# First norm of a two-block transformer kernel: the root is taken out of the input and put where products leave PSUM

## The chip, the cores and the metric

The kernel runs on one core of one Trainium2 chip. The metric is the device time of one execution in microseconds. Three executions of the kernel before gave 791.43 to 791.72 us, median 791.57 us.

## The reference, cut to what matters

Two transformer blocks follow each other, on 256 tokens of width 1024. Only the entry of the first block is touched:

```python
def rmsnorm(x, g):
    xf = x.astype(jnp.float32)
    y = xf * lax.rsqrt(jnp.mean(xf * xf, axis=-1, keepdims=True) + EPS)
    return (y * g.astype(jnp.float32)).astype(x.dtype)

u = rmsnorm(h, norm_mix_g[layer])
p = jnp.einsum('bsd,de->bse', u, w_in[layer]) + b_in[layer]
aq, ak, av, hq, hf, hi, hg, gate_a, gate_b = split_columns(p)
```

The attention branch takes aq, ak, av; the recurrent branch takes silu(hq), sigmoid(hf), hi and sigmoid(hg); sigmoid of the two gates weighs the branches. The root of a token is one factor for all columns of its row of p, so it may be applied to x or to the product.

## The kernel before

**Operands.** All products are float32 made of three fast ones: each operand is split into a rounded high part and the low rest (wH and wL of the weights, p1H and p1L of the normed input, turned so that channels lie on partitions), and wH x p1H, wH x p1L and wL x p1H are added in PSUM. ScalarE rounds the high part (split_hi, line 762, or first_hi, 776, for the first panels), VectorE subtracts it for the low part (split_lo, through the helper at line 1173).

**Panels.** A weight matrix is read in groups of 512 columns (kv has 256), each in two panels of four 128-row blocks. `timeline()` writes the order of all events out, and each engine runs through that list: at a panel, ScalarE and VectorE split the weights of the panel that comes two later (AHEAD = 2), TensorE multiplies, and at `evac` a group's tiles leave PSUM. So on VectorE the evacuation of a group stands behind the split that was listed at the group's last panel. The first groups are q0, q1, kv, ga0, ga1, hq0, hf0, hi0, hg0, gb0, gb1, hq1, hf1, hi1, hg1, then the branch products ba0, ba1 and so on; between them stand the steps of the attention (scores, scale, pt, pv) and of the recurrence (hprep, hA to hD).

**Evacuation of the first product.** Groups with channels on partitions (q, kv, hq, hf) are taken out of PSUM by ScalarE alone, with bias and function in one instruction: Identity for q (911), Identity for k and v and the shifted copy aKS of k (918), Sigmoid and Identity for hq (933, 935), two Sigmoids for hf (943, 945). Groups with tokens on partitions (hi, hg, ga, gb) are taken out by VectorE with a row of biases added (1376), and a Sigmoid on ScalarE follows for three of them.

**The entry.** SyncE loads x as two halves of 128 tokens, waits for the first, and then issues the first weights (596 to 605). ScalarE squares x and takes the roots (793, 836), TensorE turns x against the identity and spreads the roots over all partitions (1760, 1764), VectorE multiplies turned input, gain and root into TMP (1280), ScalarE rounds it to p1H (888), VectorE subtracts for p1L (1261). The order of these steps and of the first eight weight blocks is written out in the three `norm(0)`.

**Waits that matter below.** The scores of the first attention unit wait on TensorE for q1, for aKS and for aK (lines 1994 to 1996), right behind the last panel of kv. The transposes `pt` of a unit wait for its normed probabilities from VectorE. hA waits for the last product of hprep (2061). A weight slot of wH is one of three, and is free when the panel three before is done. VectorE's event `setup` prepares a small weight block dtW for the second block of the model.

Of the kernel before, what the change touches and what calls it, by code (L numbers as in the profile page):

```python
# [6 lines left out]
F32 = mybir.dt.float32  # L7
# [4 lines left out]
ALU = mybir.AluOpType  # L12
AX_X = mybir.AxisListType.X

P = 128
# [44 lines left out]
for _i in range(2):  # L60
    for _name, _c in (("q", 0), ("hq", 1280), ("hf", 2304)):
        GROUPS[f"{_name}{_i}"] = group("w_in", [(_c + _i * W, W)],
                                    cm_tiles(4 * _i if _name in ("q", "hf") else 0, 2 * _i if _name == "hq" else 0), "AAAA", "P1")
# [8 lines left out]
GROUPS["kv"] = group("w_in", [(1024, 256)], [("cm", 0, 0), ("cm", 1, P)], "AA", "P1")  # L72
# [7 lines left out]
for _name, _c in (("z", 0), ("xs", 512), ("bc", 1024), ("q2", 1544), ("k2", 2056)):  # L80
# [20 lines left out]
          "ga1": (1, 5376 + W), "hi1": (1, 3328 + W), "hg1": (1, 4352 + W)}  # L101
ROWS = 32
# [27 lines left out]
def timeline():  # L130
# [33 lines left out]
    gemm("q0")  # L164
# [47 lines left out]
def build(nc, IN, out):  # L212
# [17 lines left out]
    with ExitStack() as ctx:  # L230
# [60 lines left out]
        on.in_x = [ctx.enter_context(nc.semaphore(f"in_x{j}")) for j in range(TB)]  # L291
# [87 lines left out]
        TILE, USED, EV, SILU, SIGMOID = {}, {}, {}, {}, {}  # L379
        tiles = plain = 0  # L380
        ev = {"A": 0, "D": 0}
        for name, part in panels:
            g = GROUPS[name]
            if part == len(g["parts"]) - 1:
                for m in range(len(g["tiles"])):
# [6 lines left out]
                    if name[:2] in ("ga", "gb", "hg"):  # L392
                        ev["A"] += 1
                        SIGMOID[name, m] = (on.evac_act, ev["A"])
# [46 lines left out]
        vT, dtw, ext = scr(11, T), scr(10.5, KD, 8), scr(40, 384)[0:8]  # L441
# [53 lines left out]
        rbs = scr(69, T)  # L495

# [15 lines left out]
        HALVES = {"out1": (on.merged, 8), "down1": (on.tmp_done, 16), "oo1": (on.pt_done, 9), "dd1": EV["u9", 2]}  # L512
# [31 lines left out]
        def un(k):  # L544
            return ps[:, 4, wide(1)] if k == 7 else ps[:, 4 + k // 2, wide(k % 2)]

# [47 lines left out]
        def _(sp):  # L594
            for j in range(TB):
                sp.dma_start(res[:, j], IN["x"][0, j * P:(j + 1) * P, :]).then_inc(on.in_x[j], 16)
            sp.wait_ge(on.in_x[0], 16)
            first = IN["w_in"][0].rearrange("(k p) n -> p k n", p=P)
            for k in range(KP):
# [6 lines left out]
            for i, (kind, q) in enumerate(stream):  # L606
# [26 lines left out]
                if i == 3:  # L633
# [3 lines left out]
                    sp.dma_start(dtw, IN["w_in_2"][0].rearrange("(k p) n -> p k n", p=P)[:, :, 1536:1544]).then_inc(on.in_dtw, 16)  # L637
# [6 lines left out]
                if kind == "w" and panels[q] == ("f1", 0):  # L644
# [4 lines left out]
                    sp.wait_ge(on.hs_done, 4)  # L649
                    sp.dma_start(gfin, IN["norm_final_g"][0:1, :].partition_broadcast(P)).then_inc(on.in_gain, 16)  # L650
# [16 lines left out]
        def _(pool):  # L667
# [49 lines left out]
            for e in TL:  # L717
# [8 lines left out]
                elif e[0] == "hprep" and e[2] == 3:  # L726
                    if e[1]:
                        pool.wait_ge(on.o_psum, 2 * e[1])
                    else:
                        pool.wait_ge(on.aks, 2)  # L730
                        pool.wait_ge(on.dtw_lo, 1)
# [5 lines left out]
        def _(act):  # L737
# [50 lines left out]
            def square_x(j):  # L788

                act.wait_ge(on.in_x[j], 16)  # L790
# [59 lines left out]

            def norm(n):

                table(ACT.Sqrt)
                for j in range(TB):
# [4 lines left out]
                    elif n:  # L859
                        square(n, 1, j)  # L860
                    else:
                        square_x(j)
# [5 lines left out]
                if n == 0:  # L868
                    first_hi(0, 0, 1)
# [3 lines left out]
                for k in range(KD):  # L873
                    if n == 2 and k == 0:
                        ada_copy(1)
                    if n == 0 and 0 < k < 4:
                        first_hi(0, k, 1)
                    elif n == 0 and k in (4, 5):
                        first_hi(1, 2 * k - 8, 2)
                    elif n == 3 and 1 < k <= KP + 1:  # L880
# [5 lines left out]
                    act.wait_ge(on.tmp_done, 8 * n + k + 1)  # L886
# [15 lines left out]
            def evac(name):  # L902
# [10 lines left out]
                if g == "q" and name in ("q0", "q1"):  # L913
                    each(lambda m: aQ[:, 4 * i + m], ACT.Identity, bias=lambda m: pc("b_in", 4 * i + m))
                elif name == "kv":
                    act.wait_ge(on.tile_done, TILE[name, 0])
                    for b in range(2):
                        nc.scalar.activation(aKS[C * b:C * b + C], ps[C - C * b:P - C * b, 0, 0:T], ACT.Identity,
# [1316 lines left out]
```

## Time and profile before

| | before |
|---|---|
| time, median of 3 runs | 791.57 us |
| time of the profiled execution | 791.62 us |
| span of the profiled execution | 789.9 us |
| outside the span | 1.7 us |
| TensorE busy, share of the span | 98% |
| VectorE busy | 77% |
| ScalarE busy | 61% |
| mean granted TensorE clock | 0.999 |

The span runs from the first to the last instruction of the profile, 1.7 us lie around it. A share of busy time is a mean over stages with different limits. Matmuls overlap in the pipeline: one with 256 columns lasts 0.28 us by the profile, but starts follow each other by 0.12 us.

### The profile page before, as it was taken

How to read it: one execution, taken by the hardware profiler on the slowest of the kernel's cores; microseconds unless marked ns; L12 is line 12 of the kernel's file. 1: busy time of each engine (PE TensorE's matmuls, PEld its weight loads, DVE VectorE, ACT ScalarE, POOL GpSimd, SP SyncE). 2: the span in 40 equal slices, each digit the busy share in tenths (PEclk: the TensorE clock that was granted, in tenths of full speed). 3: DMA queues.
4: the chain of work that ended last, by engine and by line, in shares of the span. 5: the costliest groups of instructions: out<-in, count | busy, mean ns of one | idle time of the engine just before them, and what ended most of it. 6: DMA issues, size and time to landing. Idle time of an engine off the chain costs nothing. (4 is left out here: it accounts for less than half of the span.)

```text
span 789.9 us, 12522 instructions
## 1 busy us (share of the span) xinstructions
PE 776.6 (98%) x5048; PEld 686.5 (87%) x5048; DVE 606.3 (77%) x815; ACT 483.5 (61%) x733; POOL 18.0 (2%) x38
## 2 busy tenths in 40 slices
PE   8999999999999999999999999999999999999996
PEld 7978978898888898888888888999789999999885
DVE  5587787887887667887869897997878787777464
ACT  6877888468644374444334367876858667665451
POOL 3000001000200000000000000001000000000000
PEclk9999999999999999999999999999999999999999
DMA  8873634656546638799879994644363756555711
GB/s 303 295 262 126 226 124 158 189 206 219 173 161 211 213 110 273 273 306 315 274 240 339 335 372 132 230 129 139 107 213 109 239 175 200 167 171 171 240 53 54
DMA packets 106537, 162.54 MB, mean 206 GB/s; under 512 B 4576, under 2 KB 51824, under 8 KB 106480
## 3 DMA queue, kind: packets, MB, share of 16 engines
q1 hardware_dynamic: 106336, 161.48, 60.6%
q8 instruction: 40, 0.66, 0.3%
q10 hardware_dynamic: 144, 0.26, 0.1%
q14 instruction: 17, 0.14, 0.0%
HBM read 160.67 MB, written 1.06 MB: 205 GB/s over the span
## 5 line engine op out<-in xcount | busy, mean ns | idle before, releaser
L1173 DVE TENSOR_TENSOR wL<-raw,wH 128x2048 fp32r<-128x2048 f32 (+2 forms) x142 | 284.6, 2009 | 86.5 <-ACT wH L762 83.6
L762 ACT ACTIVATE wH<-raw 128x2048 fp32r<-128x2048 f32 (+1 forms) x114 | 212.0, 1863 | 86.5 <-PE ps L1864 57.7
L1861 PE MATMUL ps<-p1H,wH 128*128 128x256 f32 x784 | 223.9, 286 | 2.0 <-DVE arena L1173 0.8
L1861 PE MATMUL ps<-p1H,wL 128*128 128x256 f32 x784 | 221.2, 283 | 0.0
L1861 PE MATMUL ps<-p1L,wH 128*128 128x256 f32 x784 | 219.8, 283 | 0.0
L1861 PEld LDWEIGHTS ps<-p1H,wH 128*128 128x128 f32 x784 | 150.2, 192 | 5.7 <-issue 2.1
L1861 PEld LDWEIGHTS ps<-p1H,wL 128*128 128x128 f32 x784 | 150.2, 192 | 0.0
L1861 PEld LDWEIGHTS ps<-p1L,wH 128*128 128x128 f32 x784 | 149.5, 192 | 0.0
L1864 PE MATMUL ps<-wH,p1H 128*128 128x512 f32 x316 | 125.2, 396 | 0.0
L1864 PE MATMUL ps<-wL,p1H 128*128 128x512 f32 x316 | 123.2, 390 | 0.0
L1864 PE MATMUL ps<-wH,p1L 128*128 128x512 f32 x316 | 123.1, 390 | 0.0
L1864 PEld LDWEIGHTS ps<-wH,p1H 128*128 128x128 f32 x316 | 59.4, 188 | 12.8 <-issue 0.7
L1864 PEld LDWEIGHTS ps<-wL,p1H 128*128 128x128 f32 x316 | 59.3, 188 | 12.7
L1864 PEld LDWEIGHTS ps<-wH,p1L 128*128 128x128 f32 x316 | 59.4, 188 | 11.6
L1864 PE MATMUL ps<-wH,zH 128*128 128x512 f32 x168 | 65.4, 389 | 0.0
L1864 PE MATMUL ps<-wH,zL 128*128 128x512 f32 x168 | 65.4, 389 | 0.0
L1864 PE MATMUL ps<-wL,zH 128*128 128x512 f32 x168 | 65.4, 389 | 0.0
L1176 DVE SCALAR_TENSOR_TENSOR arena<-arena,par 128x256 f32<-128x256 f32 x116 | 47.5, 482 | 8.2 <-ACT arena L985 7.3
L1176 DVE SCALAR_TENSOR_TENSOR arena<-raw,cact,arena 128x512 f32<-128x512 f32 x56 | 42.0, 751 | 1.7
L1864 PEld LDWEIGHTS ps<-wL,zH 128*128 128x128 f32 x168 | 31.5, 188 | 6.6
L1864 PEld LDWEIGHTS ps<-wH,zH 128*128 128x128 f32 x168 | 31.5, 188 | 6.6
L1864 PEld LDWEIGHTS ps<-wH,zL 128*128 128x128 f32 x168 | 31.5, 188 | 6.4
(304 smaller groups left out, 953.3 us busy)
## 6 DMA issues: line engine op xcount, KB each, us to landing
raw<-in_w_in SPq DMA_DIRECT2D x37, 1024.0 KB, 5.8
raw<-in_w_ada SPq DMA_DIRECT2D x24, 1024.0 KB, 5.3
raw<-in_w_up SPq DMA_DIRECT2D x44, 512.0 KB, 4.7
raw<-in_w_ffn_gate SPq DMA_DIRECT2D x22, 512.0 KB, 4.4
raw<-in_w_ffn_up SPq DMA_DIRECT2D x22, 512.0 KB, 5.5
raw<-in_w_ffn_down SPq DMA_DIRECT2D x10, 1024.0 KB, 6.2
raw<-in_w_down SPq DMA_DIRECT2D x10, 1024.0 KB, 5.0
raw<-in_w_out SPq DMA_DIRECT2D x8, 1024.0 KB, 5.0
```

Of the source, the lines that this page charges most:

```text
L762: nc.scalar.activation(wH[:, q % NHL, 0:nk, 0:wd], raw[:, i % NRAW, 0:nk, 0:wd], ACT.Copy).then_inc(on.w_hi, 1)
L1173: return v.tensor_tensor(o, a, b, op)
L1176: return v.scalar_tensor_tensor(out=o, in0=a, scalar=s, in1=b, op0=op0, op1=op1)
L1861: last = mm(ps[:, t[1], 0:T], wt[:, slot, k, t[2]:t[2] + P], at_[:, k0 + k, :], start=st, stop=en)
L1864: last = mm(ps[:, t[1], 0:t[3]], at_[:, k0 + k, t[4] * P:(t[4] + 1) * P], wt[:, slot, k, t[2]:t[2] + t[3]], start=st, stop=en)
```

## The change

The input is turned and rounded with its gain but without its root; the root row is spread later and multiplied in where the products of the first matrix are evacuated.

- SyncE: x comes in four quarters of 256 channels (1 KB per token), each issued ahead of one of the first four weight blocks; the wait for x is gone. The small load dtw moves from the first loads to a place among the panels of f.
- Entry (`enter`): per 128 channels ScalarE reads the turned x from PSUM with the gain as scale into p1H, VectorE makes p1L by one scalar_tensor_tensor; the products with TMP and the root are gone. TensorE turns quarter c behind block c - 1 of q0.
- Roots (`root`): behind the first panel of q0 in the list; Sqrt table load, two squares, two roots on ScalarE. TensorE spreads them behind tile 1 of q1's first panel and then waits until ScalarE has copied the row (rb_copy) at the head of `evac q0`.
- Evacuation: q, kv, hq and hf are first multiplied by the root row on VectorE (PSUM to SBUF); ScalarE then works on SBUF. hq's bias and product become four scalar_tensor_tensor. hi, hg, ga, gb become scalar_tensor_tensor with the token's root as scalar. The scores wait for ScalarE's second step of q1 and kv, and aKS is copied last.

```diff
-GROUPS["kv"] = group("w_in", [(1024, 256)], [("cm", 0, 0), ("cm", 1, P)], "AA", "P1")
+GROUPS["kv"] = group("w_in", [(1024, 256)], [("cm", 0, 0), ("cm", 1, P)], "DD", "P1")
-    gemm("q0")
+    gemm("q0", [("root",)])
# SyncE
-            for j in range(TB):
-                sp.dma_start(res[:, j], IN["x"][0, j * P:(j + 1) * P, :]).then_inc(on.in_x[j], 16)
-            sp.wait_ge(on.in_x[0], 16)
             for k in range(KP):
+                sp.dma_start(res[:, :, wide(k)], x[:, :, wide(k)]).then_inc(on.in_x[k], 16)
                 sp.dma_start(raw[:, 0, k, :], first[:, k, 0:W]).then_inc(on.in_w0[k], 16)
# ScalarE
+            def enter():
+                act.wait_ge(on.in_par, 16)
+                for k in range(KD):
+                    if k % 2 == 0:
+                        act.wait_ge(on.ut_psum, k // 2 + 1)
+                    if k == 1:
+                        first_hi(0, 1, 1)
+                    nc.scalar.activation(p1H[:, k], xT(k), ACT.Copy, scale=gain(0, k)).then_inc(on.uh_done, 1)
+                    if k in (0, 1, 2):
+                        first_hi(0, (0, 2, 3)[k], 1)
+                    elif k in (3, 5):
+                        first_hi(1, k - 3, 2)
+            def root_0():
+                table(ACT.Sqrt)
+                for j in range(TB):
+                    square_x(j)
+                    root(0, j)
...
-                    each(lambda m: aQ[:, 4 * i + m], ACT.Identity, bias=lambda m: pc("b_in", 4 * i + m))
+                    if i == 0:
+                        act.wait_ge(on.rb_psum, 1)
+                        nc.scalar.activation(rbs0, rb, ACT.Copy).then_inc(on.rb_copy, 1)
+                    for m in range(4):
+                        act.wait_ge(*EV[name, m])
+                        nc.scalar.activation(aQ[:, 4 * i + m], aQ[:, 4 * i + m], ACT.Identity,
+                                             bias=pc("b_in", 4 * i + m)).then_inc(on.evac_act, 1)
                 elif name == "kv":
+                    for m, t in enumerate((aK, vT)):
+                        act.wait_ge(*EV[name, m])
+                        nc.scalar.activation(t, t, ACT.Identity, bias=pc("b_in", 8 + m)).then_inc(on.evac_act, 1)
+                    act.wait_ge(*SECOND[name, 0])
                     for b in range(2):
+                        nc.scalar.activation(aKS[C * b:C * b + C], aK[C - C * b:P - C * b], ACT.Copy).then_inc(on.aks, 1)
...
                     for m in range(4):
+                        act.wait_ge(*EV[name, m])
+                        nc.scalar.activation(T2[:, m], T1[:, m], ACT.Sigmoid, scale=-1.0,
+                                             bias=negb[:, 4 * i + m:4 * i + m + 1])
+                        nc.scalar.activation(T1[:, m], T1[:, m], ACT.Sigmoid,
+                                             bias=pc("b_in", 18 + 4 * i + m)).then_inc(on.evac_act, 1)
# VectorE
+                for k in range(KD):
+                    if k < 4:
+                        first_lo(0, k, 1, k == 3)
+                    elif k in (4, 6):
+                        first_lo(1, k - 4, 2, k == 6)
+                    dve.wait_ge(on.uh_done, k + 1)
+                    stt(p1L[:, k], xT(k), gain(0, k), p1H[:, k].bitcast(F32), ALU.mult, ALU.subtract).then_inc(on.u_ready, 1)
...
+                if name in ROOTED and GROUPS[name]["tiles"][0][0] == "cm":
+                    if name == "q0":
+                        dve.wait_ge(on.rb_copy, 1)
+                    for m, t in enumerate(GROUPS[name]["tiles"]):
+                        dve.wait_ge(on.tile_done, TILE[name, m])
+                        tt(to[m], ps[:, t[1], 0:T], rbs0, ALU.mult).then_inc(on.evac_dve, 1)
                 if g == "hq":
+                    for m in range(4):
+                        dve.wait_ge(*SECOND[name, m])
+                        ins = stt(hQ[:, m], hQ[:, m], pc("b_in", 10 + 4 * i + m), SQ[i][:, m], ALU.add, ALU.mult)
...
-                        tt(to, ps[:, GROUPS[name]["tiles"][j][1], :], rows(name)[0], ALU.add).then_inc(on.evac_dve, 1)
+                        stt(to, ps[:, GROUPS[name]["tiles"][j][1], :], R1[:, j:j + 1], rows(name)[0], ALU.mult,
+                            ALU.add).then_inc(on.evac_dve, 1)
# TensorE
+                        if q == 0 and k < 3:
+                            turn_input(k + 1)
+                        if (name, part, m) == ("q1", 0, 1):
+                            spread_roots(0)
+                            pe.wait_ge(on.rb_copy, 1)
...
-                        pe.wait_ge(*EV["q1", 3])
+                        pe.wait_ge(*SECOND["q1", 3])
                         pe.wait_ge(on.aks, 2)
-                        pe.wait_ge(*EV["kv", 0])
+                        pe.wait_ge(*SECOND["kv", 0])
```

## Rows read from the trace of the kernel before

**Rows 1.** Part 1 of the page: busy us, share of span, instructions.
```profile
PE 776.6 (98%) x5048; PEld 686.5 (87%) x5048; DVE 606.3 (77%) x815; ACT 483.5 (61%) x733; POOL 18.0 (2%) x38
```
**Rows 2.** Waits of TensorE: waiting line, releaser, us in total, times, longest.
```profile
PE ps L1802 <- ACT arena L911: 0.8, 1, 0.8
PE ps L1861 <- DVE p1L L1173: 0.7, 1, 0.7
```
**Rows 3.** Timeline of the opening: start us, duration, engine, line, operation.
```profile
4.31 1.06 ACT L793 ACTIVATE arena<-res 128x1024 f32<-128x1024 f32 x1 [2.00 <-DMA res<-in_x]
...
6.86 0.29 ACT L836 ACTIVATE R<-XS,eps 128x1 f32<-128x1 f32 x1
...
9.26 0.36 PE L1861 MATMUL ps<-p1H,wH 128*128 128x256 f32 x1
...
22.39 0.38 PE L1861 MATMUL ps<-p1H,wH 128*128 128x256 f32 x1
```
**Rows 4.** DMA issues of the opening: count, KB of one, median us to landing.
```profile
raw<-in_w_in SPq DMA_DIRECT2D x1, 256.0 KB, 2.7
...
raw<-in_w_in SPq DMA_DIRECT2D x2, 512.0 KB, 6.4
```
**Rows 5.** Timeline of ScalarE from 20 to 31 us, and TensorE's first scores.
```profile
20.79 1.90 ACT L762 ACTIVATE wH<-raw 128x2048 fp32r<-128x2048 f32 x1
22.59 1.55 ACT L911 ACTIVATE arena<-ps,par 128x256 f32<-128x256 f32 x4
...
25.86 1.28 ACT L1024 ACT_TABLE_LOAD   x1
...
30.41 1.04 ACT L762 ACTIVATE wH<-raw 128x1024 fp32r<-128x1024 f32 x1
...
40.68 0.59 PE L1802 MATMUL ps<-mask,identb 128*128 128x512 bf16 x2 [0.77 <-ACT arena L911]
```
**Rows 6.** VectorE's instructions of the first 60 us by form: busy us, mean ns.
```profile
L1173 DVE TENSOR_TENSOR wL<-raw,wH 128x1024 fp32r<-128x1024 f32 x9 | 10.9, 1224 | 5.8 <-ACT wH L762 5.2 <-ACT wH L758 0.5
L1173 DVE TENSOR_TENSOR wL<-raw,wH 128x2048 fp32r<-128x2048 f32 x4 | 9.2, 2292 | 3.0 <-ACT wH L762 3.0
L1173 DVE TENSOR_TENSOR p1L<-arena,p1H 128x256 fp32r<-128x256 f32 x8 | 3.4, 427 | 0.2 <-ACT p1H L888 0.2
...
L1176 DVE SCALAR_TENSOR_TENSOR acc<-raw,cact,acc 128x512 f32<-128x512 f32 x4 | 3.0, 751 | 0.1
L1173 DVE TENSOR_TENSOR wL<-raw,wH 128x512 fp32r<-128x512 f32 x4 | 2.8, 688 | 0.5 <-ACT wH L776 0.5
```
**Rows 7.** Timeline of VectorE around the evacuation of hf0.
```profile
97.47 2.29 DVE L1173 TENSOR_TENSOR wL<-raw,wH 128x2048 fp32r<-128x2048 f32 x1 [3.07 <-ACT wH L762]
...
107.27 0.69 DVE L1173 TENSOR_TENSOR arena<-arena,RD 128x512 f32<-128x512 f32 x1
```
**Rows 8.** Timeline of ScalarE and TensorE in the same stretch.
```profile
101.27 0.52 ACT L945 ACTIVATE arena<-ps,negb 128x256 f32<-128x256 f32 x1
...
108.36 1.03 PE L1760 MATMUL ps<-ident,arena 128*128 128x128 f32 x8
```
**Rows 9.** Timeline of VectorE, ScalarE and TensorE from hf1 to hA(1).
```profile
181.07 2.29 DVE L1173 TENSOR_TENSOR wL<-raw,wH 128x2048 fp32r<-128x2048 f32 x1
...
196.07 2.29 DVE L1173 TENSOR_TENSOR wL<-raw,wH 128x2048 fp32r<-128x2048 f32 x1 [2.93 <-ACT wH L762]
...
209.49 1.21 DVE L1173 TENSOR_TENSOR arena<-arena 128x1024 f32<-128x1024 f32 x1
...
185.29 1.92 ACT L762 ACTIVATE wH<-raw 128x2048 fp32r<-128x2048 f32 x1
...
211.68 1.15 PE L2071 MATMUL ps<-arena 128*64 128x64 f32 x32
```
**Rows 10.** Stretches at the end: busy us by engine, granted clock, DMA share, GB/s.
```profile
783.00:784.00 1.00, 0.60 (x6) 0.39 (x4) 0.93 (x4) 0.43 (x3) 0.00 (x0) 1.00 0.00 0
...
788.00:789.00 1.00, 0.00 (x0) 0.00 (x0) 0.00 (x0) 0.00 (x0) 0.00 (x0) 0.58 0.99 377
```

More of the change, by code:

```diff
@@ L101 @@
           "ga1": (1, 5376 + W), "hi1": (1, 3328 + W), "hg1": (1, 4352 + W)}
+ROOTED = ["kv"] + [f"{_n}{_i}" for _i in range(2) for _n in ("q", "hq", "hf", "hi", "hg", "ga", "gb")]
 ROWS = 32
@@ L290, in build @@
         on.in_rel = ctx.enter_context(nc.semaphore("in_rel"))
-        on.in_x = [ctx.enter_context(nc.semaphore(f"in_x{j}")) for j in range(TB)]
+        on.in_x = [ctx.enter_context(nc.semaphore(f"in_x{c}")) for c in range(4)]
         on.lb_diff = ctx.enter_context(nc.semaphore("lb_diff"))
@@ L495, in build @@
         rbs = scr(69, T)
+        rbs0 = dtW[:].rearrange("p k n -> p (k n)")
         adarow = TMP[:, 0:2].rearrange("p a n -> p (a n)"), scr(60, W)
@@ L788, in square_x @@
             def square_x(j):
-                act.wait_ge(on.in_x[j], 16)
+                for c in range(4):
+                    act.wait_ge(on.in_x[c], 16)
                 if j:
@@ L1472, in tail @@
                     tt(zL[:, 2 * i:2 * i + 2], zps if i in TOKENS_FIRST else ZT, zH[:, 2 * i:2 * i + 2].bitcast(F32), ALU.subtract).then_inc(on.z_ready, 1)
+                    if i == 5:
+                        dve.wait_ge(on.in_dtw, 16)
+                        step(v.memset(dtW[:], 0.0))
+                        v.tensor_copy(dtW[:, :, 0:8], dtw).then_inc(on.dtw_lo, 1)
                 elif g == "u":
@@ L1787, in late_turn, with turn_input, spread_roots @@
             def late_turn(n, k):
-                pe.wait_ge(*((on.rb_copy, n + 1) if k == 6 else (on.tmp_done, 8 * n + 2)))
+                pe.wait_ge(*((on.rb_copy, n + 1) if k == 6 else (on.tmp_done, 8 * (n - 1) + 2)))
                 turn(n, (k,), range(TB)).then_inc(on.ut_psum, 1)
+            def turn_input(c):
+                pe.wait_ge(on.in_x[c], 16)
+                if c > 1:
+                    pe.wait_ge(on.u_ready, 2 * c - 2)
+                for k in (2 * c, 2 * c + 1):
+                    for j in range(TB):
+                        last = tr(xT(k)[:, j * P:(j + 1) * P], res[:, j, k * P:(k + 1) * P])
+                last.then_inc(on.ut_psum, 1)
+            def spread_roots(n):
+                for j in range(TB):
+                    pe.wait_ge(on.rd_done, 2 * n + j + 1)
+                    last = spread(rb[:, j * P:(j + 1) * P], R1[:, j:j + 1])
+                last.then_inc(on.rb_psum, 1)
             def gate_sum(g, i):
@@ L1892, in panel @@
                         early = k == 0 and name in NORM_OF
-                        if early:
+                        if q == 0 and k == 0:
+                            pe.wait_ge(on.uh_done, 1)
+                            pe.wait_ge(on.first_hi, 1)
+                            for t in g["tiles"]:
+                                product(t, 0, only=(0,))
+                        elif early:
                             pe.wait_ge(on.uh_done, 8 * NORM_OF[name] + 1)
@@ L1905, in panel @@
                                 pe.wait_ge(on.gate_done, 2 if name == "f0" else 4)
-                            last = product(t, k, only=(0, 2) if early else (0, 1, 2))
+                            last = product(t, k, only=(2,) if early and q == 0 else (0, 2) if early else (0, 1, 2))
                         if early:
```

136 lines of the change are left out of this document (53 added, 83 removed).

## The prediction

> **What bounds the kernel now.** I read the busy shares first: TensorE 98%, VectorE 77%, ScalarE 61% [rows 1]. So TensorE is the bound, and what an edit is worth is read from TensorE's gaps. The opening timeline came next: the first product starts at 9.26 us, and q1 starts at 22.39 us [rows 3]. q0 has 96 products at a spacing of 0.12 us, 11.5 us of work, between 9.26 and 22.2 us: 1.4 us of gaps, of which TensorE's waits show 0.7 for the low part of the input [rows 2]. Then the matmul starts of the first 260 us, one after another: they follow each other without a gap, but for 0.8 us at the first scores [rows 2, 5] and 0.6 us at one pt. A gain can therefore only come from the first 22 us, and everything after it is covered by very little: each wait that is put between a last product and the next step of TensorE costs its full length. The last thing read was where VectorE and ScalarE stand in the list when a group's last tile is done, since the change puts both of them, in turn, between PSUM and the consumer.
>
> **The entry: what is gained.** x landed at 4.31 us as a half of 512 KB, and the first roots were done at 6.86 + 0.29 us [rows 3]. A load of 256 KB into an idle queue landed after 2.7 us [rows 4], so the first quarter, issued at 0.8 us, lands at 3.5; quarters and weight blocks alternate behind it at 0.3 to 0.35 MB/us, which puts the last block of q0's first panel at 9.5 to 10.2 us and the two halves of its second panel at about 11.5 and 13 us (before, these two were issued at 6.57 and 7.05 and took 6.4 us, 12.5 and 13.9 [rows 4]). ScalarE then rounds eight channel blocks (0.42 us each, by the like of p1L, 0.43 [rows 6]) and six weight pieces (0.6 or 1.05 us) and is through at 15.0 us. VectorE has four splits of 0.69 us, two of 1.22 and eight of 0.43 to 0.48 [rows 6] and follows at 16.5. TensorE works one block behind, pays 1.5 us for three groups of four turns inside q0, and ends q0 at 20.0 us instead of 22.2. **Gain 2.2 us**, between 1.2 (1 KB packets that are slower) and 3.0. A table load that now stands ahead of the first Copy could cost up to 1.28 us [rows 5], of which the loads hide most; I take nothing. TensorE's wait for rb_copy inside q1 is new: two spreads, ScalarE's copy of 0.37, and two signals of 0.15 to 0.25, together 1.1 us (0.8 if ScalarE is ready, 2 if it is late). That leaves 1.1 us gained, if nothing else stood in the way.
>
> **The chain through q0, q1 and kv: what is lost.** Before, ScalarE's work from 20.79 us on was: split for q1 (1.90), four evacuations of q0 as soon as the tiles were there (22.59, 1.55), a wait for data, a split, three table loads of 1.28 with small instructions from 25.86 to 30.41, the split for kv's second panel, the evacuations of q1, two large splits [rows 5]. It was ready just in time: TensorE waited 0.8 us and began the scores at 40.68 [rows 2, 5]. After, in the same order:
> - ScalarE: end of the entry 15.0, the two halves for q1 to 17.0, Sqrt load 1.28, squares and roots 2.84 (4.31 to 7.15 before [rows 3]) to 21.15, split for q1's second panel to 23.05.
> - VectorE splits the low part of that panel (2.29 [rows 6]) to 25.4 and only then evacuates q0, four of 0.36 to 0.43; ScalarE adds the biases behind it, to 27.5 (24.1 before).
> - Split for kv 28.5; the vectors, 4.55 us with their three loads, 33.1 (30.4 before); split 34.1. VectorE's split for kv's second panel ends at 35.3 and the evacuation of q1 at 36.8, ScalarE's biases at 37.2.
> - Two large splits, 39.05 and 40.95; VectorE's two behind them end at 41.3 and 43.5. These stand in the list before kv's evacuation.
> - VectorE takes aK out, 43.9, and v, 44.3; ScalarE biases both, 44.8, copies aKS in two halves of 0.48, 45.8; the signal to TensorE takes 0.2.
> TensorE has ended kv at 38.5 and idles until 46.0, where before it went on at 40.68. **Net loss 5.3 us**, gain and rb wait of the entry included; TensorE is not in this chain, so a faster or slower entry moves it only with ScalarE's 15.0: 4.3 to 6.5. What hides the extra evacuations before was that ScalarE had 2.2 us of waits for data and TensorE there; they are used up.
>
> **The clock.** TensorE's clock was granted in full (2.4 GHz) everywhere, also over the gaps of 0.8 us. At the end it fell to its lower level, 1.2 GHz, in the stretch from 788 us, while the last product lies in the stretch from 783 [rows 10]: some 4.7 us of idling went before it. A gap of 7.5 us is longer, so the scores and part of ga0 would run at the lower level. No row shows it rise again. Bounds: nothing, or half speed over the scores and ga0's first panel (1.7 and 5.7 us of work, up to 3.7 with the signals between). **I take 1.5 us**, the nearer end being the short one since products follow densely. The Trainium skill (TensorE: Matmul & The Clock Gate, What's actually happening) says that the throttled state is the default and activity releases it; the fall in the rows agrees, and by that rule the term cannot be nothing.
>
> **Evacuations with a scalar.** ga, gb, hi, hg: scalar_tensor_tensor of 512 columns took 0.75 us where a two-operand form took 0.69 [rows 6]: 0.1 us per group pair on the way to the probabilities of a unit; it shows only where pt already waited, after ga0: **0.2 us**. The Trainium skill (Vector Engine (DVE) Microarchitecture Reference, Points that are easy to get wrong) says scalar_tensor_tensor with two float32 sources in SBUF halves the rate; the 0.75 against 0.69, both with two such sources, does not show that. By the rule hq's four would add 1.5 us more per group.
>
> **hq0 and hf0.** hq0 costs nothing: VectorE is free to evacuate it right behind its split, ScalarE has one Sigmoid per tile instead of two instructions, and the product ends where it did. hf0 differs. VectorE's split ends at 99.76 [rows 7]; only then come four multiplies, and ScalarE's eight Sigmoids (0.36 apart) run from 100.3 to 103.2 instead of ending at 101.79 [rows 8]. Queued behind them on ScalarE are the attention output, the Exp load, half a split and the exponentials: the probabilities of unit 4, ready at 107.96 [rows 7], come at 109.2, and TensorE's second four transposes want them at 108.75 [rows 8]. **0.7 us**. The lag, less that stall, reaches unit 5: **0.4 us** (0 to 0.8).
>
> **hq1 and hf1.** hq1 is evacuated behind a split on VectorE; ScalarE's next split moves from 173.8 to 175.7, an ada step of VectorE follows, and the split at 181.07 [rows 9] moves by 1.9. hf1's multiplies start at 185.3, where ScalarE's old evacuation was already over, and ScalarE's eight Sigmoids end at 188.7: its split at 185.29 [rows 9] starts 3.4 us late. The whole chain behind it (Ln, scans, Exp, splits) is serial: the split at 196.07 moves to 199.5, ready at 201.8, for hg1's second panel that TensorE starts at 200.95 (two panels of 5.47 us ahead of hA at 211.68 [rows 9]): 1.0. ba0 0.6, and the product at 209.49 comes 3.8 late, for hA: 1.3. **2.9 us** (0.5 to 4).
>
> **Moved and hidden.** dtw's load and the making of dtW (0.5 us of VectorE) go to the stage of f, where every group waits on TensorE: nothing, up to 0.5 if a weight load behind the small packets is late. POOL loses a wait: nothing.
>
> **Sum,** against the profiled execution: span 789.9 + 5.3 + 1.5 + 0.2 + 0.7 + 0.4 + 2.9 = 800.9, with 1.7 around it 802.6; the median lies 0.05 below the profiled execution: **802.5 us**.
>
> **Rivals.**
> - The hand-offs are hidden and the entry's gain stands: 791.6 - 2.2 + 1.1 = 790.5, not slower. It decides at one point: aKS and aK must be ready when kv's last product ends, 7.3 us earlier than my chain has them. For it: ScalarE is busy only 61% [rows 1]. Against: in this stretch it has no such reserve, 0.8 us of wait stood there already. 0.09; an entry near 3.0 makes it faster by over 0.2%, which is 0.05 of it.
> - Only the first hand-off costs: VectorE's and ScalarE's slack behind it (2.93 us of waiting before 196.07 [rows 9]) takes up hf0 and hf1, and the clock costs 0.7: 791.6 + 5.3 + 0.7 = 797.6. 0.15.
> - The opening does not speed up, because quarters with 1 KB rows crowd the first weights: ScalarE's entry ends 1.5 us later and the chain with it: 804.0. 0.08.
> - The clock stays low over a whole panel more and hg1's weights cascade into the following panels: 807. 0.08.
> - My forecast: 0.60.
>
> **How the numbers follow.** The range reaches from 796.0 (second rival, with the entry's chain 1 us shorter) to 806.5 (forecast with the clock at its upper bound and the chain at its own). A change of 0.2%, 1.6 us, is about what a measurement of this kernel tells from none. Slower by over that: 0.91; within: 0.04; faster: 0.05.
>
> **What would show it.** Right: q1's first product at about 20.2 us; a pause near 23 us with ScalarE's copy behind it; TensorE idle for 6 to 8 us before the scores, released by ScalarE's copy of aKS, and VectorE's kv evacuation directly behind a split of 2.29 us; a stretch below full clock behind it; new waits at pt(4), at hg1 and at hA. Wrong: no gap over 3 us before the scores would fell the largest term, and with it the sign.

## The result, and the profile after

The changed kernel took **805.56 us** (median of 4 executions, 803.31 to 806.20) against 791.50 us before: a ratio of 1.017, 95% interval 1.0158 to 1.0183, slower by 14 us. The forecast was 802.5 with a range of 796.0 to 806.5. The profiled execution, which all traces below are read from, took 803.31 us, with a span of 801.6 against 789.9: 11.7 us longer.

The page's part 1 after the change, to be held against [rows 1] (TensorE had 776.6 us):

```profile
PE 780.3 (97%) x5044; PEld 688.8 (86%) x5044; DVE 611.7 (76%) x839; ACT 482.1 (60%) x725; POOL 22.2 (3%) x38
```

TensorE is busy 3.7 us longer with about as many instructions, and the rest is idling. Its waits, as in [rows 2] (waiting line, releaser, us in total, times, longest):

```profile
PE ps L1857 <- ACT arena L947: 6.4, 1, 6.4
...
PE ps L1916 <- ACT wH L779: 1.7, 1, 1.7
PE ps L1919 <- DVE wL L1193: 1.4, 1, 1.4
...
PE ps L1916 <- ACT dtW L936: 0.5, 1, 0.5
```

One wait of 6.4 us, for ScalarE's copy of aKS (L947), stands where 0.8 stood. The timelines of VectorE, ScalarE and TensorE around it (start, duration, engine, line, operation), which answer to [rows 5]:

```profile
40.76 4.49 DVE L1193 TENSOR_TENSOR wL<-raw,wH 128x2048 fp32r<-128x2048 f32 x2 [1.56 <-ACT wH L765]
45.17 0.75 DVE L1193 TENSOR_TENSOR arena<-ps,dtW 128x256 f32<-128x256 f32 x2
...
45.62 0.91 ACT L944 ACTIVATE arena<-arena,par 128x256 f32<-128x256 f32 x2 [3.09 <-DVE arena L1193]
46.56 0.85 ACT L947 ACTIVATE arena<-arena 64x256 f32<-64x256 f32 x2
...
47.66 1.01 PE L1857 MATMUL ps<-mask,identb 128*128 128x512 bf16 x2 [6.36 <-ACT arena L947]
```

TensorE's last product of kv starts at 41.03. Its tiles lie in PSUM while VectorE makes two splits of 2.29 us for the next weights, then VectorE takes them out, then ScalarE adds the biases, then ScalarE copies aKS. And the opening, against [rows 3]:

```profile
4.89 1.06 PE L1800 MATMUL ps<-ident,res 128*128 128x128 f32 x4
...
8.49 1.20 PE L1916 MATMUL ps<-p1H,wH 128*128 128x256 f32 x4 [1.69 <-ACT wH L779]
9.48 1.05 PE L1916 MATMUL ps<-p1H,wL 128*128 128x256 f32 x4
...
6.06 1.28 ACT L863 ACT_TABLE_LOAD   x1 [6.06 <-PE ps L1800]
7.36 0.47 ACT L863 ACTIVATE p1H<-ps,par 128x256 fp32r<-128x256 f32 x1
```

The first product starts 0.8 us earlier than before (8.49 against 9.26), but q1 starts at 22.70, 0.3 later. Four products take 1.0 us here and the next four 0.86, 0.21 to 0.25 each, where the same form is spaced by 0.12 from 11.9 us on.

### The profile page after: what moved, and what is told of

Same layout as the page of the kernel before. It is cut to its first block and busy times, and to the rows that moved or that the text cites. A ratio compares the mean times of both kernels' runs of the same rounds, so it can differ in the third digit from the quotient of the medians.

```text
span 801.6 us, 12537 instructions
## 1 busy us (share of the span) xinstructions
PE 780.3 (97%) x5044; PEld 688.8 (86%) x5044; DVE 611.7 (76%) x839; ACT 482.1 (60%) x725; POOL 22.2 (3%) x38
## 5 line engine op out<-in xcount | busy, mean ns | idle before, releaser
L1919 PEld LDWEIGHTS ps<-wH,p1L 128*128 128x128 f32 x316 | 59.6, 189 | 11.7
L1196 DVE SCALAR_TENSOR_TENSOR arena<-arena,par 128x256 f32<-128x256 f32 x124 | 50.8, 480 | 8.2 <-ACT arena L1003 7.3
```

Source lines behind the costliest of these rows:

```text
L1196: return v.scalar_tensor_tensor(out=o, in0=a, scalar=s, in1=b, op0=op0, op1=op1)
L1919: last = mm(ps[:, t[1], 0:t[3]], at_[:, k0 + k, t[4] * P:(t[4] + 1) * P], wt[:, slot, k, t[2]:t[2] + t[3]], start=st, stop=en)
```

## Experiments

Diffs are against the kernel named. The kernel before was run on the same chip each time (medians 791.59 to 791.74).

**e1_fill.** Is the slow stretch behind the gap the clock, and what is it worth? The changed kernel with 26 idle products (identity by identity) in the gap:

```diff
                     elif u:
                         pe.wait_ge(on.probs, 2 * u)
+                    if u == 0:
+                        warm(26)
                     if kind == 1:
                         pe.wait_ge(on.consts, 1)
```

> The changed kernel with 26 idle products (identity against identity) on TensorE between the last product of kv and the waits of the first scores; nothing else is touched. Theory (the clock is a term of its own): the granted clock stays at its upper level through the gap, the scores and ga0's first panel take their old times (1.8 and 5.6 us instead of 3.3 and 6.3), so the profiled span falls by about 2.2 us, to 799.4; and since the mean granted clock of the four executions of the changed kernel ran from 0.990 to 0.995 with times of 806.2 to 803.3, the spread goes too: all executions near 801. The gap itself stays, the scores start at 47.7 us. Rival (the low clock costs nothing, the spread has another cause): median 805.5, spread as before.

Measured: 803.0 us (802.77 to 803.6), ratio 1.0143 (1.0128 to 1.0158), 2.5 less than the changed kernel. The granted clock by stretch (us of the span, length, busy us of five engines, clock, DMA share, GB/s), first the changed kernel, then this one:

```profile
40.00:46.00 6.00, 1.31 (x11) 1.10 (x10) 5.16 (x4) 2.91 (x3) 0.00 (x0) 0.97 0.49 171
46.00:53.00 7.00, 5.34 (x26) 3.92 (x27) 2.13 (x5) 3.11 (x9) 0.00 (x0) 0.54 0.59 226
```
```profile
40.00:46.00 6.00, 6.00 (x55) 5.86 (x53) 5.16 (x4) 2.88 (x4) 0.00 (x0) 1.00 0.50 160
46.00:53.00 7.00, 6.14 (x40) 4.82 (x40) 3.88 (x8) 4.47 (x20) 0.00 (x0) 1.00 0.53 199
```

With the gap idle, the clock is granted at 0.54 in the stretch behind it; with the gap filled it stays at 1.00, and scores and ga0's first panel take 1.81 and 5.6 us again (3.29 and 6.29 in the changed kernel). The price of the clock in the profiled execution is shown, 2.2 us. The spread between executions, four of each, falls from 2.9 to 0.8 us, which fits that the clock made a good part of it. The scores start at 46.91 and not at the 47.7 that I expected, since q1 starts 1.1 us earlier in this execution than in that of the changed kernel, with the same opening (see e10_opening). The profiled span is only 0.6 shorter, though: the 2.4 us that stood at pt(5) were mostly used up by waits for hg1's weights (1.7 instead of 1.4), for hA (0.9, see the last section) and for a root at 487 us (0.7). My 801 was 2 us too low.

**e2_out_first.** The chain through kv: VectorE takes kv, hq and hf tiles out ahead of the split that stands before them in the list (`rooted` holds the multiplies that stood in `evac`).

```diff
+            FIRST_OUT = ("kv", "hq0", "hf0", "hq1", "hf1")
...
+                    if e[1] in FIRST_OUT and e[2] == 1:
+                        rooted(e[1])
                     if q < len(panels) and e[1:] not in LATER and e[1:] not in BESIDE:
                         split_lo(q)
```

> The changed kernel, but VectorE multiplies the tiles of kv, hq and hf out of PSUM ahead of the weight split that the list has at the group's last panel, not behind it. Theory (VectorE's queue order costs): kv's tiles come out 2.2 us earlier, so TensorE's gap ahead of the scores is 4.2 instead of 6.4 us; the stall at pt(4), 0.8 us, and the one at hg1's second panel, 1.5 us, go; with the shorter low clock median 800 to 802. Rival (ScalarE's chain through q0 and q1 alone sets all of it): at most 0.7 us less than 805.5.

Measured: 800.22 us (798.4 to 801.21), ratio 1.0104 (1.0087 to 1.0121); span 796.7.

```profile
PE ps L1866 <- ACT arena L947: 4.2, 1, 4.2
...
PE ps L1809 <- DVE arena L1193: 1.2, 4, 0.4
```

The gap is 4.2 instead of 6.4, as expected, and the wait for hg1's weights is gone. So 5.3 us of the median (4.9 of the span) came from the place of five evacuations behind a split, and not from the extra work itself. Two things limit this. Up to 0.75 us of the span is the faster opening of this execution (q1 at 21.63 against 22.70; with the same start e1_fill has its scores 0.75 earlier). And the waits at the pt steps, which I expected to lose pt(4)'s, are 1.2 us in all, four of them, where the changed kernel has 0.6. The clock falls behind this gap too: the scores take 3.10 us (44.39 to 47.49).

**e3_vectors_late.** The other piece of that chain: the small vectors with their three table loads (and the setup behind them) moved from q1 to behind ga0's first panel.

```diff
-    gemm("q1", [("vectors",)], [("setup",)])
+    gemm("q1")
-    gemm("ga0", Y(0), X(1, "ga1", 0))
+    gemm("ga0", [("vectors",), ("setup",)] + Y(0), X(1, "ga1", 0))
```

> The changed kernel with the events vectors and setup (three table loads, 4.55 us of ScalarE) moved from q1 to behind ga0's first panel. Theory (ScalarE's serial work through q0, q1 and kv sets the scores): ScalarE reaches the large splits 2.6 us earlier and is then bound by q1's and kv's products, the scores start at 45.0 instead of 47.7 us, TensorE's gap is 3.8 us, short enough for the clock to stay up: median 798.5 to 801. Rival (VectorE's splits ahead of kv's evacuation set it, ScalarE has slack): 805.

Measured: 808.41 us, ratio 1.0207 (1.0192 to 1.0222), worse than the changed kernel.

```profile
PE ps L1800 <- DVE arena L1193: 4.8, 3, 3.9
PE ps L1857 <- ACT arena L947: 4.0, 1, 4.0
```

The gap shrank to 4.0 as expected (scores at 45.77), but pt(1) now waits 3.9: the loads end at 61.1 on ScalarE, and the attention output, the Sigmoids of ga0 and the Exp load are queued behind them. The chain was read rightly and the new place badly; the expectation failed. It failed on the clock as well: I had called a gap of 3.8 us short enough, but behind the 4.0 us here the scores take 3.29 us (45.77 to 49.06), as behind the 6.4 of the changed kernel, and the clock from 46 to 51 us is granted at 0.50. Behind the 1.4 us of e7_combined they take 1.81.

**e4_entry** and **e10_opening.** Where did the entry's 2.2 us go? e4_entry puts a Sqrt table load ahead of everything and takes 3 idle products instead of 6 ahead of the first turned quarter; e10_opening also puts 8 instead of 2 behind it.

```diff
             act.wait_ge(on.pool_step, 3)
+            table(ACT.Sqrt)
...
-                        warm(6)
+                        warm(3)
                         turn_input(0)
-                        warm(2)
+                        warm(8)        # e10_opening alone; 2 in e4_entry
```

> The changed kernel with the Sqrt table loaded ahead of every wait of ScalarE, and three instead of six idle products ahead of the first turn of the input. Theory (the entry was late by the table load of 1.28 us that stood behind its waits, by the idle products that kept TensorE 1.2 us beyond the landing of x, and pays a second load at the roots): the first p1H starts at 5.7 instead of 7.4 us, ScalarE's chain is 2.9 us shorter, the scores start at 44.8, median 801 to 803. Rival (the first weights' landing bounds the entry): 805.

> The changed kernel with nothing but its opening altered: Sqrt table first, 3 idle products ahead of the first turned quarter and 8 (not 2) behind it, so that TensorE is not idle for the 1.2 to 1.7 us ahead of its first real product. Against e4_entry only the 8 differ. Theory: the opening's gain was real and was lost to the low clock; q1 starts at 21.0 (e4_entry 21.9, the changed kernel 22.7, the kernel before 22.39) and the first 12 products are 0.12 us apart. The hand-offs behind it are those of the changed kernel, so the time is 802 to 804: q1's earlier start shows in the scores by at most 1 us. Rival 'the first products wait for the rounding of their panels whatever the clock': q1 at 21.7 or later.

Measured: e4_entry 803.78 us (802.7 to 804.59), ratio 1.0147 (1.013 to 1.0164); e10_opening 802.63 (801.86 to 803.37), ratio 1.0138 (1.0124 to 1.0152). TensorE's opening, e4_entry first:

```profile
6.76 1.19 PE L1917 MATMUL ps<-p1H,wH 128*128 128x256 f32 x4 [1.24 <-ACT wH L779]
7.75 1.05 PE L1917 MATMUL ps<-p1H,wL 128*128 128x256 f32 x4
8.60 1.05 PE L1917 MATMUL ps<-p1L,wH 128*128 128x256 f32 x4
```
```profile
4.51 3.11 PE L1810 MATMUL ps<-ident 128*128 128x128 f32 x16
7.38 0.72 PE L1917 MATMUL ps<-p1H,wH 128*128 128x256 f32 x4
7.94 0.64 PE L1917 MATMUL ps<-p1H,wL 128*128 128x256 f32 x4
8.42 0.64 PE L1917 MATMUL ps<-p1L,wH 128*128 128x256 f32 x4
...
20.44 0.28 PE L1917 MATMUL ps<-p1H,wH 128*128 128x256 f32 x1
```

In e4_entry the first product starts 0.6 us sooner than in e10_opening and its twelfth product ends 0.6 later, since its products are 0.21 to 0.25 apart and not 0.12. Idle products without a gap up to the first real one bring q1 to 20.44 (21.8 in e4_entry, 22.70 in the changed kernel, 22.39 before). So of the forecast's 2.2 us 1.95 exist.

The opening differs from execution to execution, though, and each of these figures is from one. With the unaltered opening of the changed kernel q1 starts at 21.63 in e1_fill and e2_out_first, at 21.70 in e6_entry_alone, at 22.70 in the changed kernel and at 23.18 in e3_vectors_late; in the first three only about eight products are slower than 0.12. The kernel before varies less: 22.39, and 21.98 and 22.16 with the same opening in e8_before_masks and e12_before2. With 8 idle products it starts at 20.44, 20.59, 20.83 and 20.97 (e10_opening, e9_combined2, e11_combined3, e7_combined), so the two groups stay apart. Of the 2.3 us between 22.70 and 20.44, some 1.1 us is the first product's earlier start (7.38 for 8.49), and the rest is pace that three of the five executions did not lose.

e10_opening's time falls by 2.9 us against the changed kernel, within what I expected, but the scores start 2.5 us earlier (45.18 for 47.66) where I had allowed 1. e4_entry missed: scores at 46.56, expected at 44.8. Both have one reason, in ScalarE and VectorE behind q0, e4_entry first:

```profile
25.34 0.38 ACT L936 ACTIVATE dtW<-ps 128x256 f32<-128x256 f32 x1 [3.15 <-PE ps L1805]
25.76 1.42 DVE L1194 TENSOR_TENSOR arena<-ps,dtW 128x256 f32<-128x256 f32 x4 [1.25 <-ACT dtW L936]
```
```profile
23.96 0.38 ACT L936 ACTIVATE dtW<-ps 128x256 f32<-128x256 f32 x1 [2.25 <-PE ps L1805]
24.38 1.42 DVE L1194 TENSOR_TENSOR arena<-ps,dtW 128x256 f32<-128x256 f32 x4 [0.35 <-ACT dtW L936]
```

ScalarE was early, and waited for TensorE to spread the root, which stands inside q1's first panel; VectorE waited for that copy. From there on the chain to the scores hangs on TensorE: from e4_entry to e10_opening both q1 and the scores come 1.38 us earlier. In the changed kernel VectorE did not wait there (its split ended behind the copy). With the rest out of the way ScalarE's entry is bound by the weight blocks: in e10_opening it waits 2.1 us for them in four places, in the changed kernel for none.

The low pace in the opening is the clock's, by this: in e3_vectors_late, whose opening is the changed kernel's, the granted clock of the stretches 9 to 11.5 and 11.5 to 13 us is recorded below 1.

```profile
9.00:11.50 2.50, 2.50 (x16) 2.30 (x15) 2.13 (x5) 0.87 (x2) 1.21 (x4) 0.71 1.06 403
11.50:13.00 1.50, 1.50 (x9) 1.50 (x9) 0.95 (x2) 1.49 (x4) 0.00 (x0) 0.50 1.04 386
```

**e5_handoff_alone** and **e6_entry_alone.** The change in two halves. e5: the kernel before, its own entry and root, with the changed kernel's hand-offs; VectorE multiplies by a tile of ones that stands for the spread root:

```diff
+                    step(v.memset(dtW[:], 1.0))
                     turn_over(n, 0)
...
+                    for m, t in enumerate(GROUPS[name]["tiles"]):
+                        dve.wait_ge(on.tile_done, TILE[name, m])
+                        tt(to[m], ps[:, t[1], 0:T], rbs0, ALU.mult).then_inc(on.evac_dve, 1)
```

e6: the changed kernel's entry, late root and spread, with the evacuations of before; nothing multiplies by the root.

> The kernel before, with its own entry and its own root before the first product; only the evacuations are the changed kernel's (VectorE multiplies out of the banks by a tile that holds 1.0 everywhere, ScalarE follows in place, aKS is copied from the tile instead of from the bank, the gates keep the tensor_tensor of before). The output is the reference's. Theory: the second engine behind the attention tiles is the whole loss. Scores start at 45.5 to 46.5 instead of 40.68, TensorE's gap ahead of them is over 5 us and the granted clock falls once behind it; with 2.2 for the clock, 0.85 at pt(4) and 1.5 to 2 around hf1 and hA the time is 800 to 802. Rival 'the entry and the late root make part of it': 795 to 798, scores below 44. Rival 'the hand-off is hidden': 791.6 to 792.5.

> The other half alone: input in channel quarters, turned and rounded without its root, the root computed and spread inside q1 and copied by ScalarE behind q0; but the evacuations are those of the kernel before and nothing multiplies by the root (the output lacks it). Theory: the entry gains nothing (q1 starts at 22.4 to 22.9 against 22.39) since its first products run at the low clock, and the spread and its wait, 1.07 us on TensorE in q1, are mostly covered by the 1 us gap ahead of the scores: 791.6 to 793, scores at 41.0 to 41.8. Rival 'the entry is worth its 2.2 us where no hand-off follows': scores at 39.6 to 40, 790.0 to 790.5. Rival 'the entry is a loss by itself': 795 or more.

Measured: e5 802.04 us (801.45 to 802.26), ratio 1.0125 (1.011 to 1.014), span 799.9; e6 793.23 (791.99 to 794.43), ratio 1.0018 (1.0008 to 1.0027), span 790.3. TensorE's longest wait in e5:

```profile
PE ps L1811 <- ACT arena L925: 5.8, 1, 5.8
```

Scores start at 45.55 in e5 and 41.07 in e6. The hand-offs alone cost 10.0 us of span, the entry alone 0.4, both 11.7. Of the remaining 1.3, 0.75 is the opening of the profiled executions: q1 starts at 21.70 in e6 and at 22.70 in the changed kernel, and e1_fill, with it at 21.63, has the scores of the changed kernel 0.75 earlier. The other 0.5 may be that in e6 the later root and squares fall into ScalarE's slack, which in the changed kernel the hand-offs have used; this was not tested apart. By medians the halves cost 10.3 and 1.5 us and both 14.0. So the entry alone is a small loss clear of the noise, more than the 0.4 of its profiled execution, which was among the fastest of ten, and just outside the 793 that I had as its upper end.

**e7_combined, e9_combined2, e11_combined3.** Can the idea be made to pay? Everything found so far together: e2's order, e10's opening, the vectors' Sigmoids moved to ga0's own and their Silu and Exp behind kv, the spread one tile earlier, aKS copied ahead of v's bias. e9: only kv, hq1 and hf1 out first; the wait for the root's copy ahead of q1's fourth tile; the scores' masks ahead of the wait for aKS; the setup behind the first scores. e11 is e9 with ext, one piece of that setup, ahead of the scores again.

```diff
-    gemm("q1", [("vectors",)], [("setup",)])
+    gemm("q1")
-    gemm("kv", [], first[:-1] + [("v_turn",)] + first[-1:])
+    gemm("kv", [], [("vectors",), ("setup",)] + first[:-1] + [("v_turn",)] + first[-1:])   # e7, e11
+    gemm("kv", [], [("vectors",)] + first[:-1] + [("v_turn",)] + first[-1:])               # e9
-    gemm("ga0", Y(0), X(1, "ga1", 0))
+    gemm("ga0", Y(0), [("sign",)] + X(1, "ga1", 0))                                        # e7, e11
+    gemm("ga0", Y(0), [("setup",), ("sign",)] + X(1, "ga1", 0))                            # e9
```

> The changed kernel with everything that the runs pointed to: VectorE takes kv, hq and hf tiles out ahead of the split of the next weights; ScalarE's Sqrt table ahead of the entry and 3 idle products instead of 6, 8 instead of 2 behind the first turned quarter (to keep the clock up until the first product); the spread of the root one tile earlier in q1; the vectors' two Sigmoids moved to ga0's Sigmoids, their Silu and Exp and the setup behind kv's evacuation, where ScalarE idled 3.6 us; aKS copied ahead of vT. Theory: q1 starts at 20.5 to 21.5 (full clock from about 7 instead of 11.5), kv's products end at 40 to 40.5 and the scores start within 1 us of it; no low stretch of the clock behind kv; what is left is 0.9 at pt(4), 1 around hA, 0.2 for the gates: 790.5 to 793, that is level with the kernel before. Rival 'low clock of the opening is bound by idle time before 2.2 us, not by the gap': q1 at 21.9, 792 to 794. Rival 'the moved vectors collide with the Exp of the first scores': ga0 or its pt waits 1 to 2 us, 794 to 796.

> e7_combined with four repairs: only kv, hq1 and hf1 are taken out ahead of the split (in e7_combined TensorE waited 0.5 and 0.6 us in pt(3) and pt(4) for VectorE, which took hq0 and hf0 out first); the setup stands behind the first scores instead of ahead of them (it made VectorE 0.4 us late for their maximum); the wait for the root's copy stands ahead of q1's fourth tile instead of right behind the spread (0.47 us); the scores' masks are added ahead of the wait for aKS (0.6 us of the 1.4 us gap). Theory: 0.9 + 0.4 + 0.5 + 0.6 = 2.4 less than e7_combined's 794.7: 792.3, range 791.5 to 793.2, level with or 0.2% behind the kernel before. Rival 'the waits only move': 794 to 795.

> e9_combined2 with one thing put back: the part of the setup that makes ext stands ahead of the first scores again, since in e9_combined2 SyncE's queue of loads waited for it (ext_done) and stood still from 46 to 55 us (DMA share 0.01, TensorE waited 3.8 us in pt(1)); the rest of the setup stays behind the first scores. Theory: the 3.8 us and what they set off go: e9_combined2 stood 0.2 ahead of the kernel before at 54 us, and picks up 0.7 at pt(4) and 0.3 to 1 after it: 791.8 to 793, still not below the kernel before. Rival 'the late rest of the setup delays pt(0) as it did in e7_combined': 794 or more.

Measured: e7 794.69 us (794.06 to 794.88), ratio 1.0033 (1.0021 to 1.0045); e9 798.46, ratio 1.0085 (1.0071 to 1.0098); e11 793.21 (792.31 to 796.16), ratio 1.0024 (1.0014 to 1.0034). e9 missed by 6 us. A stretch of it, and the wait of the queue that issues the loads:

```profile
46.00:51.00 5.00, 4.02 (x21) 2.95 (x21) 4.64 (x9) 4.06 (x11) 0.00 (x0) 1.00 0.02 3
51.00:56.00 5.00, 5.00 (x36) 3.64 (x36) 4.89 (x6) 2.72 (x5) 0.00 (x0) 1.00 0.01 2
...
SPq L646 <- DVE arena L1578: 18.7, 1, 18.7
...
62.52 1.06 ACT L773 ACTIVATE wH<-raw 128x1024 fp32r<-128x1024 f32 x1 [3.49 <-DMA raw<-in_w_in]
```

SyncE stores ext and waits for it (L646) ahead of the next weights; with ext made behind the first scores, next to nothing was loaded for 10 us (DMA share 0.02 and 0.01) and ScalarE stood 3.5 us at 62 us. e11, which puts back that one piece, shows it: 5.3 us less. (e3_vectors_late had the same stall, 20.6 us at that wait and a DMA share of 0.01 from 46 to 61 us; there ScalarE was late by itself and hid it from me.) e11 still stands 1.5 us behind the kernel before: it starts the scores' products at 39.90, 1.3 us ahead of the 41.20 before, and loses the lead at the pt steps, where TensorE waits 2.2 us in all for VectorE, 0.3 and 0.7 of them in pt(0); before, 0.6. e7 came out above its expected 790.5 to 793: TensorE waits 1.4 us ahead of the scores and 2.0 at the pt steps.

**e8_before_masks** and **e12_before2.** Do the finds help the kernel before? e8 moves the masks of the first scores ahead of the wait for aKS, e12 also the vectors and the setup, much as in e7.

```diff
                         pe.wait_ge(*EV["q1", 3])
+                        if u == 0:
+                            masks(u)
                         pe.wait_ge(on.aks, 2)
...
-                    if u == 0:
-                        masks(u)
```

> The kernel before with one edit: the two mask products of the first scores stand ahead of TensorE's wait for aKS and aK instead of behind it. They take 0.5 to 0.6 of the 0.8 us gap. Theory: 791.0 to 791.3, 0.5 us (0.06%) less than before, at the edge of what can be measured. Rival 'the scores end no earlier, since VectorE or ScalarE is late behind them': 791.6.

> The kernel before with the two edits that helped the changed one and that need nothing of it: the scores' masks ahead of the wait for aKS, and the vectors' table loads (three, 1.28 us each) out of ScalarE's way between q1 and kv. Theory: the 0.3 us that e8_before_masks still waited goes too, and the time is 790.6 to 791.0, 0.1% below the kernel before. Rival 'the moved table loads make the first Exp late': 791.5 to 792.5, worse than e8_before_masks.

Measured: e8 791.07 us (790.6 to 791.44, 11 executions) against 791.67, ratio 0.9993 (0.9984 to 1.0002), as expected, and by its interval not told from no change; its median is the lowest here. e12 792.42 (792.15 to 793.88), ratio 1.001 (1.0001 to 1.0019): its rival was right. Its scores start no later, and the first Exp comes at 44.67 instead of 44.08: the moved table loads push ScalarE's next split, VectorE waits 1.37 us for that, and pt(0) waits for VectorE:

```profile
44.87 1.23 DVE L1174 TENSOR_TENSOR wL<-raw,wH 128x1024 fp32r<-128x1024 f32 x1 [1.37 <-ACT wH L770]
...
48.84 0.66 PE L1762 MATMUL ps<-ident,arena 128*128 128x128 f32 x4 [0.67 <-DVE arena L1174]
```

## Why the prediction was right, and where its sizes were off

The sign, the largest term and its mechanism were right: TensorE idled 6.4 us ahead of the scores, released by the copy of aKS, with the evacuation of kv right behind a split, as the forecast had listed it. Step by step, as offsets against the kernel before in the profiled execution:

| step | forecast | measured | from |
|---|---|---|---|
| entry, before the spread | -2.2 | +0.3 | q1 22.70, before 22.39; -0.7 to -0.8 and +0.8 in other executions |
| spread and wait for its copy | 1.1 | 1.1 | 25.58 to 26.66 |
| scores start, both included | 5.3 | 7.0 | 47.66, before 40.68 |
| clock behind the gap | 1.5 | 2.2 | scores 3.29 for 1.81, ga0 6.29 for 5.57 |
| ga0's gates, pt(1) | 0.2 | -0.5 | a wait of 0.6 that was there before shrank |
| hf0, pt(4) | 0.7 | 0.9 | 117.36, before 108.36 |
| pt(5) | 0.4 | 0.1 | |
| hg1's second panel | 1.0 | 1.5 | wait of 1.37 at 211.89 |
| ba0 and hA | 1.9 | 0.5 | 223.34, before 211.68 |
| span | 11.0 | 11.7 | 801.6, before 789.9 |

- **The entry's gain was mis-sized: 2.2, measured nothing in this execution** (between 0.8 won and 0.8 lost in the five profiled ones with this opening). The step that failed is "I take nothing" for the table load, and that no term stood for the clock. The load stands behind ScalarE's wait for the turned quarter and not ahead of it, 6.06 to 7.34; six idle products keep TensorE until 4.89, when the quarter could be turned at 3.6 (as e4_entry does); and TensorE then idles 1.69 us and runs its first products at half pace. I had assumed full pace from the first product. e10_opening removes these three and gets q1 at 20.44, near the 20.2 of the forecast. ScalarE's entry ended at 16.5, 1.5 later than my 15.0. That is the third rival, with its size, although not with its cause: ScalarE waited for no load there. Its 804.0 lies between the profiled execution and the median.
- **The chain** came out 1.7 too short for this reason almost alone: from ScalarE's 15.0 my list has 31.0 us to the scores, the trace 31.1 from 16.5. "TensorE is not in this chain" held in this execution only by 0.3 us: ScalarE waited 1.59 us for the spread of the root, and its copy ended at 26.60, just before VectorE was through with its split at 26.95. In e4_entry and e10_opening TensorE is in it. And ScalarE's waits of 2.2 us before are 2.8 in the trace, 0.64 of them for a load.
- **The clock** was mis-sized twice: 2.2 in the profiled execution, and probably more in the others, whose mean granted clock is 0.992, 0.990 and 0.990 against 0.995. The median lies 2.3 us above the profiled execution, where I had taken 0.05 below; how much of this belongs to the gap and how much to the opening was not traced. e1_fill, with no low stretch behind kv, has a spread of 0.8 us. The bound of 3.7 was itself wrong: half speed over 1.7 + 5.7 us of work costs another 7.4, not half of it. Behind the gap the first products of ga0 are 0.42 us apart, later ones 0.23; that the cost stayed at 2.2 is because full pace was back early in ga0's first panel.
- **hf0 and hg1** were right within 0.5. **hA** was too high by 1.4: VectorE's subtraction ahead of it took 1.22 us and not the 3.42 of before (last section), so 2.2 us of delay vanished there. In e1_fill and e10_opening, where it took 3.42, TensorE waits 0.9 at hA.
- **The first rival** (hand-offs hidden) and **the second** (only the first costs) fall: e5_handoff_alone costs 10.0 us by itself, 3.7 of them behind the start of pt(0) (54.37 against 48.06).

So the span was near by luck, because errors had opposite signs: entry and clock 2.4 too low and hf0 and hg1 0.7, but pt(1), pt(5) and hA 2.4 too high (0.7, 0.3 and 1.4). The median is 3.1 above the forecast, 0.7 of it from the span and 2.3 from the other executions. The ends of the range do not follow from my own terms either: with the clock at 3.7 and the chain at 6.5 the upper end is 805.9 and not 806.5, and the second rival less 1 us is 796.6 and not 796.0; the measured 805.56 is inside both ways, close to the upper end. Of the loss, 10.0 us are the second engine between PSUM and its consumer (e5_handoff_alone), and about half of this is only the order: the evacuation stood behind a split (e2_out_first).

## What to carry to other kernels

Where one engine is 98% busy, an engine's mean load says nothing on whether an added hand-off is hidden: write out what stands in each queue from the last product to the next, ahead of the evacuation too, and let the engine that takes tiles out of PSUM do that before it prepares the next weights. A gain in an opening has to be counted at the pace that its first products really have; keep the array busy until they start. Whoever moves small setup work counts the DMA queue that waits for its result: it stalled all loads for 10 us here.

## What the runs showed of the hardware

**The page's clock and the products' pace can differ in the opening.** In the changed kernel the granted clock of 7 to 12 us is given as 1.00, while its products are 0.21 to 0.25 us apart, about twice the usual 0.12; in e3_vectors_late, with the same opening, it is 0.71 and 0.50 as quoted above. Executions of the same opening differ in when full pace comes (q1 at 21.63, 21.63, 21.70, 22.70 and 23.18), so read the pace off the starts of equal products, and an opening off more than one execution. The Trainium skill (TensorE: Matmul & The Clock Gate, What's actually happening) says that the low state is the default and is left by activity; e4_entry against e10_opening, which differ by six idle products and have their first real ones 0.25 and 0.14 us apart, agrees.

**VectorE and GpSimd delay each other by whole instructions, and which one is delayed varies.** VectorE has a subtraction and GpSimd a product of 128x1024 here, each with both inputs in SBUF. VectorE's and GpSimd's timelines, before the change and after it:

```profile
203.94 3.42 DVE L1173 TENSOR_TENSOR arena<-arena 128x1024 f32<-128x1024 f32 x1
...
201.87 4.41 POOL L725 TENSOR_TENSOR arena<-arena 128x1024 f32<-128x1024 f32 x1 [63.83 <-DVE arena L1173]
```
```profile
217.54 1.22 DVE L1193 TENSOR_TENSOR arena<-arena 128x1024 f32<-128x1024 f32 x1
...
215.46 8.88 POOL L729 TENSOR_TENSOR arena<-arena 128x1024 f32<-128x1024 f32 x1 [67.66 <-DVE arena L1193]
```

Either VectorE's subtraction takes 3.42 and GpSimd's 4.41, or 1.22 and 8.88; no other pair was seen in the fourteen traces (3.42 in twelve, 1.22 in the changed kernel and e11_combined3). In both cases GpSimd starts 0.1 us behind a split of VectorE. In the first, VectorE's instruction ends 1.1 us behind GpSimd's end; in the second, GpSimd ends 2.2 us behind VectorE's third instruction in a row. Both fit that one holds something for its whole instruction and the other stands still. The Trainium skill (SBUF — State Buffer, SBUF: two separate sides) says that the two engines share a port pair as an exclusive lock, taken for a whole instruction by whichever starts first; a VectorE instruction takes part where it has two inputs in SBUF and the GpSimd one reads SBUF. The sizes agree, and that a row of VectorE's instructions can pass a waiting GpSimd one is what the second pair adds. That it is this lock was argued from the times, not tested.
